# The riding products of differential attention's sample part, in other portions

## The reference

```
q, k, v : 8 heads; q and k of a head are two maps of 64 columns each
k_all = concat(cached k of the stream, new k);  v_all likewise
p = softmax(q . k_all * 64**-0.5 + T5 bias)      for each of the two maps
w = p[map 0] - lambda * p[map 1]
out = rmsnorm(w . v_all) * gain
```

## Time and profile before

| | |
|---|---|
| median of three timed runs | 3284.94 us |
| the profiled execution, its own time | 3285.09 us |
| span from its first to its last instruction | 3283.3 us |
| TensorE busy | 3127.9 us, 95% of the span |
| VectorE, ScalarE, GpSimd busy | 42%, 34%, 26% |
| mean granted TensorE clock | 0.98 of full speed |

### The profile page before, as it was taken

One profiled execution on the slowest core, in us unless ns is written; L12 is line 12 of the kernel. 1 busy time (PEld: TensorE's weight loads), 2 busy tenths in 40 slices (PEclk: granted clock), 3 DMA queues, 4 the chain that ended last, 5 costly groups with the idle time before them and its releaser, 6 DMA issues. The chain is left out here.

```text
span 3283.3 us, 50029 instructions
## 1 busy us (share of the span) xinstructions
PE 3127.9 (95%) x19550; PEld 2946.4 (90%) x19550; DVE 1384.2 (42%) x1453; ACT 1131.1 (34%) x1594; POOL 862.8 (26%) x515
## 2 busy tenths in 40 slices
PE   7899999999999999999688989999989999999997
PEld 6899999999988888888477879999979999999996
DVE  5554444544335555555432331222044444444443
ACT  5244433444234444444332330222142222222222
POOL 2333233332211211212002221334323222222220
PEclk9999999999999999999899999999989999999998
DMA  5311221121258776877756654432211111111101
GB/s 148 92 53 54 61 66 54 46 68 54 61 113 156 142 115 141 154 133 145 132 116 158 148 180 143 147 103 74 67 58 45 38 45 38 45 38 38 38 26 69
DMA packets 684752, 295.69 MB, mean 90 GB/s; under 512 B 350524, under 2 KB 665436, under 8 KB 684680
## 3 DMA queue, kind: packets, MB, share of 16 engines
q1 hardware_dynamic: 680232, 285.90, 36.2%
q10 hardware_dynamic: 4448, 8.80, 0.7%
HBM read 240.23 MB, written 54.41 MB: 90 GB/s over the span
## 5 line engine op out<-in xcount | busy, mean ns | idle before, releaser
L119 POOL TENSOR_TENSOR weight_lo<-weight_stage,weight_hi 128x1024 fp32r<-128x1024 f32 x180 | 457.5, 2542 | 1365.1 <-ACT weight_hi L114 1364.9
L1939 PE MATMUL group<-h_hi_part,weight_hi 128*128 128x384 f32 x1056 | 359.8, 341 | 12.6 <-POOL weight_lo L119 7.9
L166 PE MATMUL group<-h_hi_part,weight_hi 128*128 128x384 f32 x984 | 348.9, 355 | 17.7 <-DVE key_rows L727 5.2
L1940 PE MATMUL group<-h_lo_part,weight_hi 128*128 128x384 f32 x1056 | 359.5, 340 | 0.0
L1941 PE MATMUL group<-h_hi_part,weight_lo 128*128 128x384 f32 x1056 | 359.3, 340 | 0.0
L114 ACT ACTIVATE weight_hi<-weight_stage 128x1024 fp32r<-128x1024 f32 x180 | 190.9, 1061 | 417.9 <-PE group L2206 244.0
L167 PE MATMUL group<-h_lo_part,weight_hi 128*128 128x384 f32 x984 | 334.0, 339 | 0.0
L168 PE MATMUL group<-h_hi_part,weight_lo 128*128 128x384 f32 x984 | 333.9, 339 | 0.0
L2204 PE MATMUL group<-h_hi_part,weight_hi 128*128 128x384 f32 x768 | 259.7, 338 | 7.2 <-PEq L1551 7.2
L2205 PE MATMUL group<-h_lo_part,weight_hi 128*128 128x384 f32 x768 | 258.8, 337 | 0.0
L2206 PE MATMUL group<-h_hi_part,weight_lo 128*128 128x384 f32 x768 | 258.8, 337 | 0.0
(11 more groups left out here) (352 smaller groups left out, 6570.7 us busy)
## 6 DMA issues: line engine op xcount, KB each, us to landing
weight_stage<-in_w_in SPq DMA_DIRECT2D x88, 512.0 KB, 4.8
cached_v<-in_cache_diff_v SPq DMA_DIRECT2D x128, 256.0 KB, 5.0
cached_k<-in_cache_diff_k SPq DMA_DIRECT2D x224, 128.0 KB, 4.2
weight_stage<-in_w_up SPq DMA_DIRECT2D x44, 512.0 KB, 3.9
gate_in<-scratch_gates SPq DMA_DIRECT2D x24, 576.0 KB, 3.8
weight_stage<-in_w_branch SPq DMA_DIRECT2D x24, 512.0 KB, 4.0
down_stage<-in_w_down SPq DMA_DIRECT2D x22, 512.0 KB, 3.6
scratch_gates<-gate SPq DMA_DIRECT2D x16, 576.0 KB, 4.1
```

What stands on the lines that cost most here:

```text
L119: pool.tensor_tensor(self.wlo[:, n % 2, :], self.wst[:, n % 2, :], self.whi[:, n % 2, :].bitcast(F32), ALU.subtract).then_inc(self.w_lo, 1)
L166: pe.matmul(out, wh[:, k, :], xh[:, k, cols], start=(k == 0), stop=False)
L1939: pe.matmul(o, w[0][:, k, :], ahi[:, k, rows], start=(k == 0), stop=False)
L1940: pe.matmul(o, w[0][:, k, :], alo[:, k, rows], start=False, stop=False)
```

## The change

The 64 riding products of the sample part stay the same products in the same order. Only the places change at which the other work is put between them. The portions were 16, 8, 16, 8, 8 and 8, and are 21, 5, 19, 5, 8 and 6. In the old portions the pieces end with the first, the third and the last portion. In the new ones piece 9 ends after 16 of the 21 products of the first portion, and piece 10 after 14 of the 19 products of the third.

```diff
                 turn(NQ)
                 sample_scores(0)
-                ride(9 * STEPS + 8, 10 * STEPS)
+                rest = 9 * STEPS + 8
+                ride(rest, rest + 21)
                 sample_turn(0)
-                ride(10 * STEPS, 10 * STEPS + 8)
+                ride(rest + 21, rest + 26)
                 sample_out(0)
                 sample_scores(1)
-                ride(10 * STEPS + 8, 11 * STEPS)
+                ride(rest + 26, rest + 45)
                 sample_columns(0)
                 sample_turn(1)
-                ride(11 * STEPS, 11 * STEPS + 8)
+                ride(rest + 45, rest + 50)
                 sample_out(1)
-                ride(11 * STEPS + 8, 11 * STEPS + 16)
+                ride(rest + 50, rest + 58)
                 sample_columns(1)
-                ride(11 * STEPS + 16, 12 * STEPS)
+                ride(rest + 58, rest + 64)
```

## The result

The changed kernel is slower by a little: 3290.62 us against 3283.76 us (medians of 20 runs each). The ratio is 1.0021, with a 95% interval of 1.0013 to 1.0028, that is 6.9 us (4.3 to 9.2). The forecast was 8.4 us more. TensorE is as busy as before, and still at 95% of a longer span.

The account below looks back on a forecast made before the run. TensorE, busy 95% of the span, was taken as the bound, so its waits lengthen the kernel. Per head 0 + 1.40 - 0.35 = 1.05 us, times 8 = 8.4 us, on 3284.94 gives 3293.3 us; range 3289 to 3298.

Parts of the forecast that it names:

- First portion: Ahead of sample_turn(0): five products of piece 10 wait for ScalarE's copy of piece 9, starting it 1.26 us later.
- Second and fourth portion: From sample_turn to sample_out in both halves: three riders less save nothing, since ScalarE sets the 2.40 us.
- the prediction's sign for it: Ahead of each sample_out: TensorE would wait about half a microsecond in the changed kernel's timeline.
- The scores and the keys: Second half's scores: start 1.26 us later, find 1.95 us of slack behind late keys, end unmoved at no cost.
- nothing is absorbed: Rival, 6%: last keys come later by as much as TensorE, first half's 1.26 us paid too; 3303.4 us.
- the keys come earlier: Rival, 8%: values' loads start later, last keys land 0.7 us sooner per head; 3287.8 us, no change.
- The fourth stream: Rival, 12%: in the second half's scores it queues behind the other three, 0.6 us a head more; 3298.1 us.
- One sign: At the scores' weight loads (L1425): the wait for keys would shrink by about 1.26 us a head.
- Third portion: Ahead of sample_turn(1): five riders wait for the copy of piece 10 behind the exponentials, starting it 1.40 us later.
- The tail: Fifth and sixth portions, before MS: the last is two riders shorter, 0.35 us less a head.
- Sum: All sample parts: 0 + 1.40 - 0.35 = 1.05 us a head, 8.4 us over eight heads.
- The clock: Rival, 5%: TensorE's longer stops in the sample part lower its clock once a head, 16 us more; about 3309 us.

Follow-up runs that it names:

- early_copy: Changed kernel, but ScalarE copies piece 10 ahead of the second half's exponentials instead of behind them; ratio 1.0003 to the kernel before.
- first_half: Kernel before with only the first half's portions changed (21, 5, 14, 8, 8, 8); ratio 0.9997.
- thirty: Kernel before with portions 30, 5, 5, 8, 8, 8, so 14 products of piece 10 stand ahead of sample_turn(0); ratio 1.0041.
- second_half: Kernel before with portions 16, 8, 19, 5, 8, 8, so only the second half crosses a piece's end; ratio 1.0029.

## Why the prediction was right

*First portion.* Forecast 1.26 us later at `sample_turn(0)`, behind the copy; measured 10.2 us in eight heads, 1.27 each.

*Second and fourth portion.* Forecast: nothing saved, as ScalarE sets the distance to `sample_out`. It is 2.36 to 2.38 us with five riders in most heads, 2.40 with eight; `early_copy` and `first_half`, each with a portion of five, have 2.36 to 2.39. The idle time that the missing riders leave ahead of `sample_out` is 0.35 us; the prediction's sign for it was about half a microsecond.

*The scores and the keys.* This was where I had to choose. The end stayed 1.88 us behind the last keys, although the last stream started amid the others, and the stretch became 9.8 us shorter for 9.9 us of later start (10.20 at `sample_turn(0)`, less the 0.34 by which the way to `sample_out(0)` is shorter). `first_half` shows that no loss is left, `thirty` that it returns when the slack is used up. From the first L1427 to the second the eight heads together take 100.3 us before and 100.4 after, so the last keys came neither later with TensorE nor earlier, which answers two of the rivals, that nothing is absorbed and that the keys come earlier.

The fourth stream doesn't queue behind the others. In the second head the first stream starts at 1105.77 and the last has its keys at 1106.45; by the trace's records, in which a stream's four products start about 0.43 us apart, those of the last stream start at 1106.50, 1106.95, 1107.38 and 1107.81, and the last products of the other three only at 1107.06 to 1107.10. In the kernel before, all twelve products of these three had started by 1105.65 and the last stream's first one came at 1106.31, so the order among the streams isn't fixed. The Trainium skill, "TensorE: Matmul & The Clock Gate", Part 3, The mechanism, states that matmuls start and end in program order. The measurement decides against that rule here.

One sign was put too high: the wait of the scores' weight loads for keys shrank by 0.94 us a head (8.3 to 0.8 us in all) and not by 1.26. It was only 1.04 us a head before, since for part of the 1.95 us of slack TensorE still ran the other streams' products. The sum goes by the slack and not by this wait.

*Third portion.* Forecast 1.40 us later at `sample_turn(1)`; measured 1.43 to 1.45 in the heads of the loop, 11.6 in all. It is the change's whole loss: `second_half` alone has it, and `early_copy` takes half of it away by the copy's place alone.

*The tail.* Forecast 0.35 us a head less; measured 2.81 us in eight.

*Sum.* Forecast 8.4 us; measured 8.55 in the profiles and 6.9 (4.3 to 9.2) in the timed runs. Each term came out near its forecast, so the sum isn't right by errors that cancel. The difference is below the 9.9 us that the prediction took as the least that can be told from no change; with 20 runs of each kernel the interval leaves no change out all the same.

Of the rivals, none decided. The clock didn't fall in the changed kernel's profile, where TensorE stopped for about 1.04 and 1.40 us in the heads of the loop: the granted clock of the second head is 1.00 behind the second stop, and so it is in the other seven.

```profile
1111.00:1112.60 1.60, 0.25 (x2) 0.00 (x0) 0.32 (x2) 1.60 (x3) 0.00 (x0) 1.00 1.17 302
1112.60:1116.00 3.40, 3.17 (x21) 2.85 (x21) 0.01 (x1) 1.24 (x2) 0.00 (x0) 1.00 0.68 186
```

But such a fall was nearer than I had put it. My row for one came from the last head of the kernel before, with TensorE much less busy and behind a stop of 3.39 us:

```profile
1594.85 1.23 PE L1400 MATMUL group<-diff_k,diff_q 64*128 64x256 f32 x4 [3.39 <-ACT probs L1144]
```

The experiments have falls behind stops of 2.0 us. Each cost about 1.5 us there, where the prediction had put 2.

## What to carry to other kernels

Work that is put into a wait must be free to run there: before moving products across the end of an accumulation, look who empties the bank and what stands ahead of that copy in the engine's own order. A delay costs only as much as the next late arrival leaves over, so the two halves of one edit can have quite different prices; cut the timeline at the points that several engines share and compare stretch by stretch. To gain by filling a gap, take the filler from a stretch whose length the filler itself sets.

## What the runs showed of the hardware

TensorE's clock fell behind short stops in an otherwise busy stretch. Ahead of `sample_turn(1)` the stops in the second head were 1.63, 2.0, 2.33 and 2.5 us in four kernels, and the slow stretch followed in 0, 4, 5 and 7 of eight heads, one profiled execution each. In `second_half` the clock also fell behind a stop of 2.17 us ahead of the last stream's scores, in the eighth head. In a head in which it happened, riders started 0.32 us apart in place of 0.17, the granted clock was 0.53 behind the stop (`thirty`), and the way from `sample_turn(1)` to `MS` took about 1.5 us longer (in `thirty` 4.02 + 5.30 us in the second head, where before it is 2.41 + 5.41). Why some heads of one kernel fall and others not, with stops alike to a few hundredths, these runs don't tell; in `thirty` the first and the eighth head stopped for 2.56 us each, and the clock fell in the first alone.

Score products of different streams, each stream on 32 partitions of its own, passed each other: in the changed kernel's second head the last stream's first product started at 1106.50, ahead of the last products of the three streams that stand before it in the program (1107.06 to 1107.10), and the sixteen took no longer behind the last keys than one stream alone, 1.88 us.
